# Block 2's gate weights loaded earlier, and eight queries of a mixture-of-experts layer half a step to a step earlier, in a two-block kernel on one core

## What is computed

```python
q = (xt @ w_q).reshape(TOKEN_BLOCK, PEER_HEADS, 2, PEER_HALF_DIM)
sc = jnp.einsum('thcd,chnd->thcn', q, sub_keys)
top_s, top_i = lax.top_k(sc, k)
...
pre = jnp.einsum('td,thkd->thk', xt, u[idx])
coef = (g * jax.nn.gelu(pre, approximate=False)).astype(v.dtype)
return jnp.einsum('thk,thkd->td', coef, v[idx])
```

```python
proj = (hn @ w_in).astype(jnp.float32)
fq, fk, fv, ff, mq, mk, mv, mi, mf, mo, bq, bk, bv = jnp.split(proj, idx, axis=-1)
```

## Time and profile before

| | us |
|---|---|
| median of 3 runs | 2631.87 |
| lowest, highest of them | 2614.95, 2632.45 |
| the profiled execution's own time | 2619.42 |
| its span, first to last instruction | 2617.6 |
| PE busy, share of the span | 2099.7 (80%) |
| DVE busy | 1729.6 (66%) |
| POOL busy | 1038.7 (40%) |
| 512 + 512 gathers of rows, bytes | 536.94 MB of 676.48 MB |

### The profile page before, as it was taken

How to read it: one execution, slowest core, us unless ns; L and a number is a source line. 1 busy time by engine, 2 the same in 40 slices (tenths; PEclk the granted TensorE clock), 3 DMA queues, 4 the chain that set the end, 5 groups by cost and what they waited for, 6 DMA issues and landing times. The chain is left out here.

```text
span 2617.6 us, 25392 instructions
## 1 busy us (share of the span) xinstructions
PE 2099.7 (80%) x7625; PEld 1323.9 (51%) x7625; DVE 1729.6 (66%) x3556; ACT 605.0 (23%) x1394; POOL 1038.7 (40%) x1083
## 2 busy tenths in 40 slices
PE   4985857878776867877799678776968798899999
PEld 4963544444332333434454333333428664788877
DVE  4956438988787776677667588778747462544465
ACT  2134213332222211122112132222221221111121
POOL 0000015666666667676557566667740000000000
PEclk8995888999897988888899888889988887899999
DMA  5741038999999999999999899999984200333222
GB/s 178 279 160 65 17 129 284 372 343 377 342 362 392 366 368 391 406 390 377 361 371 401 314 386 360 353 357 369 379 280 145 99 1 10 106 94 95 80 81 96
DMA packets 266857, 676.48 MB, mean 258 GB/s; under 512 B 25725, under 2 KB 114162, under 8 KB 266738
## 3 DMA queue, kind: packets, MB, share of 16 engines
q0 software_dynamic: 147456, 536.94, 54.2%
q1 hardware_dynamic: 119282, 138.13, 15.9%
HBM read 672.87 MB, written 2.10 MB: 258 GB/s over the span
## 5 line engine op out<-in xcount | busy, mean ns | idle before, releaser
L2183 PE MATMUL bank<-arena 128*128 128x512 f32 x1536 | 817.8, 668 | 158.0 <-DMA arena<-in_peer_v,arena 85.5
L2413 DVE SCALAR_TENSOR_TENSOR arena<-arena,h_ps 128x1024 f32<-128x1024 f32 x512 | 613.1, 1217 | 171.9 <-DMA arena<-in_peer_u,arena 130.9
L2146 POOL DMA_INDIRECT arena<-in_peer_v,arena x512 | 511.0, 998 | 358.3 <-issue 138.8
L2146 POOL DMA_INDIRECT arena<-in_peer_u,arena x512 | 512.4, 1001 | 215.8 <-issue 147.9
L2183 PEld LDWEIGHTS bank<-arena 128*128 128x128 f32 x1536 | 305.1, 212 | 512.1 <-issue 363.9
L2426 DVE SCALAR_TENSOR_TENSOR x<-arena,x 128x1024 f32<-128x1024 f32 x128 | 164.6, 1286 | 45.0 <-DMA arena<-in_peer_v,arena 27.7
L1453 PE MATMUL bank<-hT,arena 128*128 128x256 f32 x512 | 129.1, 408 | 31.2 <-DMA arena<-in_peer_w_q 24.9
L2267 ACT ACTIVATE arena<-ident,arena 128x128 f32<-128x128 f32 x384 | 135.8, 393 | 69.3 <-issue 33.2
L142 DVE CAST parts<-arena 128x2048 fp32r<-128x2048 f32 (+4 forms) x60 | 68.1, 1136 | 112.9 <-DMA arena<-in_w_gate_up 71.8
L1453 PEld LDWEIGHTS bank<-hT,arena 128*128 128x128 f32 x512 | 105.0, 207 | 62.1 <-DMA arena<-in_peer_w_q 26.3
L144 DVE TENSOR_TENSOR parts<-arena,parts 128x2048 fp32r<-128x2048 f32 (+4 forms) x60 | 126.7, 2111 | 4.5
(11 more groups left out here) (413 smaller groups left out, 3348.0 us busy)
## 6 DMA issues: line engine op xcount, KB each, us to landing
arena<-in_w_in SPq DMA_DIRECT2D x16, 1536.0 KB, 6.7
arena<-in_w_ada SPq DMA_DIRECT2D x12, 2048.0 KB, 9.8
arena<-in_w_gate_up SPq DMA_DIRECT2D x44, 512.0 KB, 4.9
arena<-in_peer_w_q SPq DMA_DIRECT2D x16, 1024.0 KB
arena<-in_w_down SPq DMA_DIRECT2D x22, 512.0 KB, 3.5
arena<-in_peer_u,arena POOLq DMA_INDIRECT x512
arena<-in_peer_v,arena POOLq DMA_INDIRECT x512
arena<-in_w_in SPq DMA_DIRECT2D x8, 1024.0 KB
```

The source lines that it names most:

```text
L2146: nc.gpsimd.indirect_dma_start(out=ring[:, n % R, :], out_offset=None, in_=a[table][0], in_offset=bass.IndirectOffsetOnAxis(ap=expert[:, s ...
L2183: ins = nc.tensor.matmul(psum[half][:, :], diag[:, m % R, :], v_ring[:, n % R, half * 512:(half + 1) * 512], start=(s % PH == 0 and j == 0 ...
L2413: nc.vector.scalar_tensor_tensor(out=u_ring[:, n % R, :], in0=u_ring[:, n % R, :], scalar=1.0, in1=h_ps[:, :], op0=ALU.mult, op1=ALU.mult, ...
```

## The change

- Query 8 runs in the second half of step 11 (slots 8 and 11, `half_scores` at 13); queries 9 to 15 run in steps 12 to 18 at the slots they had.
- The gate weights `w_g_a` lie in `q_T` (the buffer of the turned queries) and no longer in X2. DVE zeroes them at the start of tile 2 after the last `half_scores`. Their three narrow loads are issued by SP between the loads of tiles 4 and 5, on a semaphore of their own.
- Tile 8's 256 further columns are loaded like any other tile, after tile 6.
- SP's list has all query loads first, then tiles 2, 3, 4, the gates, 5 to 9.
- Both `o2_add` of token blocks 0 and 1 stand three slots later.

```diff
-            return [(i - 12 + PH, 1)] if 0 <= i - 12 < PH else []
+            return [(i - 11 + PH, 8 if i == 11 else 1)] if 0 <= i - 11 < PH else []
...
-        w_g_a, w_mq_a = view(X2, KD, 2 * NG), view(X2 + KD * 2 * NG, KD, ML_W)
+        w_g_a, w_mq_a = view(Q_T, KD, 2 * NG), view(X2, KD, ML_W)
+        w_g_loaded = sem("w_g_loaded")
...
         def load_w_2(sync, t):
+            after(sync, in2_summed, t - 1)
             if t == 8:
-                sync.wait_ge(gates_zeroed, 1)
-                for c0, n, at in ((FF0, FOX_H, 0), (MF0, ML_H, MF), (MI0, ML_H, NG + MF)):
-                    sync.dma_start(w_g_a[:, :, at:at + n], w_in_2[:, :, c0:c0 + n]).then_inc(w_2_loaded[0], 16)
                 sync.dma_start(w_mq_a, w_in_2[:, :, MQK0:MQK0 + ML_W]).then_inc(w_2_loaded[0], 16)
                 return
-            after(sync, in2_summed, t - 1)
...
+        def load_w_g(sync):
+            sync.wait_ge(gates_zeroed, 1)
+            for c0, n, at in ((FF0, FOX_H, 0), (MF0, ML_H, MF), (MI0, ML_H, NG + MF)):
+                sync.dma_start(w_g_a[:, :, at:at + n], w_in_2[:, :, c0:c0 + n]).then_inc(w_g_loaded, 16)
...
                 pe.wait_ge(w_2_loaded[t % 2], w_2_count(t))
+                if t == 8:
+                    pe.wait_ge(w_g_loaded, 48)
...
+            if slot == I0 + 2 * KD:
+                dve.wait_ge(sc_summed, 2 * PH)
+                nc.vector.memset(w_g_a, 0.0).then_inc(gates_zeroed, 1)
             if slot == I0 + 7 * KD:
-                dve.wait_ge(in2_summed, 7)
-                nc.vector.memset(w_g_a, 0.0).then_inc(gates_zeroed, 1)
...
-            if slot == O2_0 + KD + 1:
+            if slot == O2_0 + KD + 4:
                 o2_add(dve, 0, 0, psum[4:6])
-            if slot == O2_0 + 2 * KD + 1:
+            if slot == O2_0 + 2 * KD + 4:
                 o2_add(dve, 0, 1, psum[6:8])
...
-                    if Q == 2 * PH - 2:
-                        load_w_2(sync, 2)
-                for t in range(3, len(TILES_2)):
+                for t in range(2, len(TILES_2)):
+                    if t == 5:
+                        load_w_g(sync)
                     load_w_2(sync, t)
```

More of the change, by code:

```diff
@@ L1547, in load_w_2 @@
         def load_w_2(sync, t):
+            after(sync, in2_summed, t - 1)
             if t == 8:
-                sync.wait_ge(gates_zeroed, 1)
-                for c0, n, at in ((FF0, FOX_H, 0), (MF0, ML_H, MF), (MI0, ML_H, NG + MF)):
-                    sync.dma_start(w_g_a[:, :, at:at + n], w_in_2[:, :, c0:c0 + n]).then_inc(w_2_loaded[0], 16)
                 sync.dma_start(w_mq_a, w_in_2[:, :, MQK0:MQK0 + ML_W]).then_inc(w_2_loaded[0], 16)
                 return
-            after(sync, in2_summed, t - 1)
             c0, n = TILES_2[t]
             sync.dma_start(tile_2(t), w_in_2[:, :, c0:c0 + n]).then_inc(w_2_loaded[t % 2], 16)
+        def load_w_g(sync):
+            sync.wait_ge(gates_zeroed, 1)
+            for c0, n, at in ((FF0, FOX_H, 0), (MF0, ML_H, MF), (MI0, ML_H, NG + MF)):
+                sync.dma_start(w_g_a[:, :, at:at + n], w_in_2[:, :, c0:c0 + n]).then_inc(w_g_loaded, 16)
         def w_2_count(t):
-            return 16 * (t // 2 + 1 + (3 if t == 8 else 0))
+            return 16 * (t // 2 + 1)
         def load_w_out_a(sync, i):
@@ L2108, in block2_dve @@
                 gate_apply(dve, 0, ml_gain_a)
-            if slot == O2_0 + KD + 1:
+            if slot == O2_0 + KD + 4:
                 o2_add(dve, 0, 0, psum[4:6])
-            if slot == O2_0 + 2 * KD + 1:
+            if slot == O2_0 + 2 * KD + 4:
                 o2_add(dve, 0, 1, psum[6:8])
-        assert C0 + O2_0 + 2 * KD + 1 <= (STEPS + 1) * PK
+        assert C0 + O2_0 + 2 * KD + 4 <= (STEPS + 1) * PK
         with nc.Block() as block:
@@ L2516, in program @@
         w_high, w_low = ([{n: view_r(at + d, KD * n) for n in (384, ML_W, 2 * NG + ML_W)} for at in part_at] for d in (3072, 0))
-        w_split, loaded_by = sem("w_2_split"), [16 * 8, 16 * 5]
+        w_split, loaded_by = sem("w_2_split"), [16 * 5, 16 * 5]
         def width_b(i):
```

## The result

The changed kernel's median is 2606.3 us (2598.2 to 2622.51, 20 runs) against 2628.18 us (2614.55 to 2636.66, 20 runs): a ratio of 0.994, 95% interval 0.9922 to 0.9958, or 11 to 20 us less; the two medians lie 21.9 us apart. Forecast were 2611 us and a gain of 13.9. The changed kernel was compared twice more with the kernel before, in later sets of runs: 0.9956 (0.992 to 0.9992) and 0.9944 (0.9912 to 0.9976). An interval behind a ratio is a 95% interval throughout.

A forecast was written before the change was run, and what follows sets the result against it. The DMA engines were taken to bound the expert loop. Terms -5.1 - 14.1 + 5.3 = -13.9 us from the profiled 2619.42 gave 2605.5, or 2611 us on the scale of the runs; range 2596 to 2626 us.

The forecast's parts named there:

- Loop DMA-bound, stalls priced in missing bytes: Expert loop: DMA engines bound it, no compute engine is full; every stall is priced by bytes missing against 403 GB/s.
- Query 15, -5.1: Query 15, issued a step earlier and no longer behind tile 2: its 8.41 us weights wait goes, gaining 5.1 us.
- Tile 8, -14.1: Tile 8, its 256 columns issued when tile 6 ends: the 20.67 us wait goes, gaining 14.1 us.
- The new stall, +5.3: Tile 5, behind the narrow loads: PE stalls 13.5 us, gap 17.3, loss 5.3 us (bounds 2.3 to 8.9).
- loss = gap - 12: PE's `v` sums: some 12 us of a gap are covered by gathers already issued; loss is the rest, never below 0.
- 3120 packets one for one with gathers: Three narrow loads between tiles 4 and 5: 3120 packets alternate with gather packets at 104 per us, taking 29.9 us.
- Query 8 in step 11, 0: Step 11: the same matrix products moved cost nothing; PE may wait 0 to 5 us for the next query's load.
- `o2_add`, 0: `o2_add` three slots later: taken as 0, since a wait on PE would show PE as its releaser.
- the rival's 4.69 us: DVE's pause ahead of the second `o2_add` goes too, with the narrow loads hidden: -23.9 us in all, chance 0.03.
- hidden: Tile 5: narrow loads cost nothing, the free part being over 12 us; -19.2 us, 2600.2 or 2605 us, chance 0.22.
- given back: Loop: stalls go, but it is later held up elsewhere by as much; net 0, 2625 us, chance 0.15.
- slower: Tile 5: narrow packets pass at only 76.8 per us, 40.6 us; net +0.4 to +0.8 us, 2625 us, chance 0.08.

The follow-up runs named there:

- two spread narrow loads: Changed kernel with two narrow loads (6 and 8 columns) instead of three, one ahead of tile 5, one ahead of tile 6: 2513.12 us, ratio 0.9944 to the kernel before.
- all four changed kernels: Changed kernel with no narrow loads, two spread, three with old `o2_add` slots, or six: 2513.3, 2513.12, 2518.6 and 2522.41 us.
- the one with three narrow loads: Changed kernel with both `o2_add` of token blocks 0 and 1 at their old slots: 2518.6 us, ratio 0.9964 to the kernel before.
- third set: Changed kernel, one narrow load ahead of each of tiles 5 to 7, two ahead of tile 5: 2606.16, 2601.46, 2603.25 us; kernel before 2625.4.
- second set: Changed kernel with none, two, three (old `o2_add` slots) and six narrow loads, against the kernel before at 2528.88 us: ratios 0.9939, 0.9944, 0.9964, 0.9972.
- six loads: Changed kernel with each narrow load issued twice, the second time into unused columns: 2522.41 us, ratio 0.9972 to the kernel before.
- no narrow loads: Changed kernel without the three narrow loads, gates computed from zeros: 2513.3 us, ratio 0.9939 to the kernel before.
- fourth sets: Fourth set: the kernel before against itself, 2529.82 against 2528.49 us, ratio 1.0005.
- the spread version: Changed kernel with one narrow load ahead of each of tiles 5, 6 and 7: 2597.18 us, ratio 0.9915 to the kernel before; later 2601.46 us, 0.9908.
- the first and the fourth set: First: changed kernel 2612.19, queries only 2617.62, gates only 2618.89, narrow loads ahead of tiles 5 to 7 2597.18 us. Fourth: kernel before against itself, ratio 1.0005.

## Why the prediction was right

Both long waits went, the new one came at the forecast place, for the forecast cause and by the counted packets. The sum came within 3 us by marks and within 2 by the first ratio. Part of that closeness is luck: some sizes were off and offset each other, and one reason was wrong. The forecast of 2611 us was 5 above the measured median; the medians lie 8 us further apart than the forecast gain, and the comparisons that followed have 11.5 and 14.7 us by their ratios. Point by point:

**Loop DMA-bound, stalls priced in missing bytes.** Held: with every stall gone the stretch runs at 403 GB/s (401 with two spread narrow loads), and the kernels with stalls are at 369 to 395.

**Query 15, -5.1.** The wait is gone, and marks 19 to 22 give 5.2; in bytes it had cost 5.8 us in one profile of the kernel before and 8.1 in the other. What the prediction had not counted is on the other side: marks 10 to 19 are 2.6 to 3.1 us longer in all four changed kernels. The DMA queues between these marks, the kernel before and then the one with three narrow loads:

```profile
q0 software_dynamic: 41210, 150.07, 94.6%
q1 hardware_dynamic: 9478, 10.05, 7.1%
```

```profile
q0 software_dynamic: 41371, 150.64, 94.2%
q1 hardware_dynamic: 10403, 10.98, 7.7%
```

925 packets and 0.93 MB more: nearly one query load, moved ahead of mark 19. From mark 19 to 24 the same queue has 925 packets fewer (11369 for 12294). With 0.57 MB more of gathers that is 1.5 MB, 3.7 us at 403 GB/s; the kernel with two spread loads has 0.92 MB more of loads and no more gathers, 2.3 us, for its 2.6. Where DMA is the bound, moved bytes move their time. This reading rests on the packet counts; no run takes the move apart from the rest. By it about 3 of the 5.2 us are only moved, and by marks the queries' part is worth some 2 us net. The term of the sum was mis-sized by what it left out: it priced the wait that goes, and not the load that now falls into an earlier stretch. The run with the queries' part alone (0.9967, 0.9928 to 1.0006) can't tell 2 us from 5.

**Tile 8, -14.1.** The wait for the weights is gone in every kernel with the gates' part; what is left ahead of tile 8 names ACT (1.74 us) or no releaser (1.64, and 4.21 in the third set). 14.4 and 14.9 us in bytes in the two profiles of the kernel before, so the price in missing bytes was right; the 16.3 by marks hold 1.7 us of bytes that fell into this stretch.

**The new stall, +5.3.** The place, the cause and the length of the wait held: tile 5, for a weights' load, 15.73 us in the first profile and 12.5 to 13.0 in three others, against 13.5 (bounds 10.5 to 17.1). Its loss by windows is 5.4 us in the first profile; in the second set all three narrow loads cost 1.9 by marks and 4.9 by bytes, the packets' own 1.2 included. The gap was 20.9 us in the first profile, at which the rule "loss = gap - 12" says 8.9: the free part is nearer 15 here (20.9 - 5.4), and 27.7 - 13.1 = 14.6 with six loads. So the first profile's 5.4 for 5.3 is luck: a gap 3.6 us longer than forecast, and 3 us more of it free. Where the gap was as forecast (17.3), the loss by marks was under 2, and the term was too large. Why more is free here than at the two waits of before was not settled.

**3120 packets one for one with gathers.** Held (424 against 425), and shown to go by count and not by bytes: same bytes in 2080 packets, 0.81 us of wait in place of 12.51. The Trainium skill's "DMA: Bandwidth & Descriptors", section "Why small descriptors are slow (HBM only)", prices a small packet by about three cycles and 32 bytes of metadata; by the estimate from it (1.1 us for all three loads) there would have been no stall, and the trace does not agree as long as gathers are in the other queue. The same page's section "Queues, rings and completion order" says that an engine goes round the queues that have work for it, typically some 9 to 17 descriptors at a time. The equal counts in the 4 us windows with both queues full agree with going round, and the 799 packets in one us once the gathers ran out agree with passing over a queue that has none; how many go in one turn no row here shows.

**Query 8 in step 11, 0.** PE waits up to 4.8 us for the next query's weights, inside the 0 to 5 forecast (PE, no narrow loads):

```profile
923.90 5.41 PE L1453 MATMUL bank<-hT,arena 128*128 128x256 f32 x16 [4.78 <-DMA arena<-in_peer_w_q]
```

It is free, as taken: the window 914:962 has 400 GB/s around it. In the slower sets step 11 showed something else, below.

**`o2_add`, 0.** The 0 held; the rival's 4.69 us were no gain to be had. The reason given did not hold: it read a pause with no releaser shown as proof that DVE did not wait for PE, and DVE does wait for PE at the old slots, 2.40 us in the changed kernel and 2.35 in the kernel before. It costs nothing because the step is no longer for it.

**Sum.** By marks 10 to 24 in the second and fourth sets: 5.2 + 16.3 - 1.9 = 19.6 us won, less 3.1 moved ahead, is 16.5 (670.99 - 654.50), where the forecast was 13.9. The ratio of the first comparison says 15.8 (11 to 20). What doesn't fit: that kernel's own runs show 9.1 us (4 to 14) for these 16.5. Its profiled execution was the lowest of its 12, 2509.2, and the marks come from that one; the rest of the difference stays open. The rivals: "hidden" is out for the first profile, whose windows lack 5.4 us, and nearly right by marks in the later ones (0 to 1.7 us against the spread version from mark 20 to 22, 0.7 from 19 to 24 in the second set); "given back" is out as a whole, though 3 of 19.6 us are moved ahead; "slower", with narrow packets at 76.8 per us, is out by 424 in 4 us.

## What to carry to other kernels

When DMA sets the time, price a wait by the bytes that go missing, and price a load that stands in front of another by its packets, beside whatever the other queues hold: 56 KB in 3120 packets took 30 us to pass, and the next tile's load stood behind them. Put such a load where its successor has slack, one piece per gap, or make it of fewer and wider packets; either took this wait away, and by the marks most of a wait of 12 to 13 us had cost nothing. Moving a load earlier in a DMA-bound stretch moves its time along with it, as far as the packet counts here show, so read a gain over the whole stretch and not from the one step in which a wait vanished.

## What the hardware showed beyond that

- Sets of runs differ by more than the change is worth: the kernel before took 2623.1, 2528.9, 2625.4 and 2528.5 us in the four, a spread of 3.8%. It is not shown to be a matter of the chip: the first and the fourth set bear the same chip number, 5, and lie 95 us apart. In the fast sets most loop steps of different kernels agree within some tenths of a us; in the slow ones marks 1 to 10, which the change leaves alone, took 426 to 454 us (398 to 400 in the fast ones), which blurs differences of this size.
- In the slower sets and in the first profile ACT stood still in step 11 of the changed kernel ahead of a query's copy, with no releaser shown (21.08 to 24.27 us), and PE waited 5.34 to 8.16 us for it. ACT, then PE, in the first profile:

```profile
963.38 0.58 ACT L1460 COPY arena<-bank 128x512 f32<-128x512 f32 x1 [24.27 <-remote]
```

```profile
964.41 3.65 PE L2189 MATMUL bank<-arena 128*128 128x512 f32 x4 [8.16 <-ACT arena L2273]
```

  PE's query had ended at 954.5. That step took 53.3 us for 42.3 before, and the next two were 3.7 and 4.7 shorter. From mark 10 to 14 the changed kernel took 186.7 to 192.3 us against 189.5, so nothing of it is left. With the queries' part alone the step was short (42.6 us) but the one ahead of it long (52.7 for 47.9), and marks 10 to 14 took 190.7. In the fast set it does not occur (41.9 to 42.1 us, and ACT's wait names PE). Its cause is open.
- Issuing a load can block SP: the three narrow ones took 24.66 us to issue right behind tile 4's (six took 53.25), and 10.45 in the kernel before, where no load stood ahead of them. Tile 5's load was issued at 1352.33, long before the packets ahead of it had passed, so this cost nothing here.
